# Attention scores over 64 rows, even and odd head back to back, with the attention pipeline stepped in pairs of units

## The reference

```
# layer 0 (DSA): 12 heads of 64, one shared k and v, mask "score" from an indexer
s = einsum('bthd,btkd->bthk', q, k) * 64 ** -0.5
p = masked_softmax(s, mask);  o = einsum('bthk,btkd->bthd', p, v)
# layer 1 (NSA): 12 heads in 2 groups, three branches for each head
o = g0 * att(q, k_cmp, v_cmp)      # 31 compressed keys
  + g1 * att(q_rot, k_s, v_s)      # causal, up to 512 keys
  + g2 * att(q_rot, k_w, v_w)      # causal, up to 512 keys
# both layers: 4 more heads over 256 memory positions
x = x + concat(tok, o_mem) @ w_o
```

## Time and profile before

| | |
|---|---|
| median of 3 runs | 3527.47 us (3523.74 to 3528.39) |
| profiled execution, its own time | 3527.51 us |
| span in its trace | 3525.7 us |
| PE busy in the span | 3348.1 us (95%) |
| DVE, ACT, POOL busy | 47%, 42%, 45% |
| attention of layer 0 | from 208.65 us to about 292 us |
| attention of layer 1 | from 857.8 us to about 1061 us |
| granted TensorE clock in both | 1.00 and 0.98 of full |

### The profile page before, as it was taken

How to read it: one execution, slowest core, us unless ns; L and a number is a source line. 1 busy time by engine, 2 the same in 40 slices (tenths; PEclk the granted TensorE clock), 3 DMA queues, 4 the chain that set the end, 5 groups by cost and what they waited for, 6 DMA issues and landing times.

```text
span 3525.7 us, 46614 instructions
## 1 busy us (share of the span) xinstructions
PE 3348.1 (95%) x16902; PEld 2768.0 (79%) x16902; DVE 1657.1 (47%) x2719; ACT 1472.4 (42%) x2771; POOL 1601.7 (45%) x1404
## 2 busy tenths in 40 slices
PE   6899999999999999999989996899999999999998
PEld 4578888877778888788877775788888878888886
DVE  4784433142773332343326876555565552333321
ACT  3355433223664333333325554454445542243322
POOL 4245544662445445544553321444444435464454
PEclk8899999997999999999999997999999999999999
DMA  4111333341002333333332220111111113333332
GB/s 122 42 43 49 95 95 97 94 115 37 1 1 84 95 95 94 95 98 95 94 86 62 59 54 25 37 43 37 42 37 37 39 46 96 96 96 95 98 96 70
DMA packets 471315, 245.93 MB, mean 70 GB/s; under 512 B 13820, under 2 KB 468711, under 8 KB 471015
## 3 DMA queue, kind: packets, MB, share of 16 engines
q1 hardware_dynamic: 470144, 241.33, 24.1%
q10 hardware_dynamic: 998, 2.30, 0.2%
HBM read 241.51 MB, written 2.10 MB: 69 GB/s over the span
## 4 chain that ended last, share of the span: by engine, by line
PE 85%; DVE 8%; ACT 3%; issue 2%; POOL 1%; DMA 0%; ACTq 0%; DVEq 0%; POOLq 0%
PE ps L463 18%; PE ps L464 18%; PE ps L465 18%; PE ps L1545 3%; PE ps L1525 3%; PE ps L2281 2%; PE ps L2177 2%; PE ps L2179 2%; PE ps L2178 2%; PE ps L2263 2%; PE ps L1534 2%; PE ps L1696 1%; PE ps L1697 1%; PE ps L1698 1%; PE ps L1769 1%
## 5 line engine op out<-in xcount | busy, mean ns | idle before, releaser
L445 POOL TENSOR_TENSOR w_lo<-ring,w_hi 128x512 fp32r<-128x512 f32 (+1 forms) x908 | 1223.8, 1369 | 1540.6 <-ACT w_hi L436 1540.6
L436 ACT ACTIVATE w_hi<-ring 128x512 fp32r<-128x512 f32 (+1 forms) x908 | 516.1, 617 | 1276.5 <-PE ps L465 1191.8
L463 PE MATMUL ps<-h_hi,w_hi 128*128 128x512 f32 x1776 | 701.7, 395 | 4.4 <-POOL w_lo L445 4.4
L465 PE MATMUL ps<-h_hi,w_lo 128*128 128x512 f32 x1776 | 691.9, 390 | 0.0
L464 PE MATMUL ps<-h_lo,w_hi 128*128 128x512 f32 x1640 | 638.8, 390 | 0.0
L463 PEld LDWEIGHTS ps<-h_hi,w_hi 128*128 128x128 f32 x1776 | 333.8, 188 | 80.7 <-POOL w_lo L445 6.4
L465 PEld LDWEIGHTS ps<-h_hi,w_lo 128*128 128x128 f32 x1776 | 333.7, 188 | 69.8
L464 PEld LDWEIGHTS ps<-h_lo,w_hi 128*128 128x128 f32 x1640 | 308.4, 188 | 68.5 <-issue 5.0
L464 PE MATMUL ps<-a_lo,w_hi 128*128 128x512 f32 x752 | 292.5, 389 | 0.0
L465 PE MATMUL ps<-a_hi,w_lo 128*128 128x512 f32 x720 | 280.1, 389 | 0.0
L463 PE MATMUL ps<-a_hi,w_hi 128*128 128x512 f32 x720 | 280.1, 389 | 0.0
(11 more groups left out here) (445 smaller groups left out, 6195.1 us busy)
## 6 DMA issues: line engine op xcount, KB each, us to landing
ring<-in_ffn_w_in SPq DMA_DIRECT2D x176, 512.0 KB, 3.8
ring<-in_w_in SPq DMA_DIRECT2D x96, 512.0 KB, 4.0
ring<-in_ffn_w_down SPq DMA_DIRECT2D x32, 512.0 KB, 3.7
ring<-in_ffn_w_out SPq DMA_DIRECT2D x32, 512.0 KB, 3.6
ring<-in_w_o SPq DMA_DIRECT2D x16, 512.0 KB, 3.7
ring<-in_w_branch_gdn SPq DMA_DIRECT2D x16, 512.0 KB, 3.6
ring<-in_nsa_w_in SPq DMA_DIRECT2D x15, 512.0 KB, 3.8
ring<-in_dsa_w_in SPq DMA_DIRECT2D x13, 512.0 KB, 4.1
```

The lines of the kernel that those rows point to most:

```text
L436: act.activation(w_hi[:, (halves(u) + j) % PIECES, 0:n, :], slot(u)[:, j * n:(j + 1) * n, :], ACT.Copy) \
L445: pool.tensor_tensor(w_lo[:, q % PIECES, 0:n, :], slot(u)[:, j * n:(j + 1) * n, :], w_hi[:, q % PIECES, 0:n, :].bitcast(f32), ALU.subtract ...
L463: pe.matmul(dst, wh, hi(k), start=first and k == 0, stop=False)
L465: ins = pe.matmul(dst, wl, hi(k), start=False, stop=last and k == 2 * n - 1)
```

## The change

On TensorE the contraction of a score product shrinks from 128 rows to the head's own 64 (`even_odd[n % 2]`), for all units, the compressed and the memory ones too. The even and the odd head of a pair are issued one right behind the other, so in layer 1 the order of units becomes: tile, branch, head. TensorE and ScalarE go on in steps of two units: TensorE's step i issues S of both units of pair-step i, T of both of i-2, and V of both of i-3, key tile by key tile, even and odd in turn; ScalarE's step i is both exponentials of i and then both copies of i-2. VectorE keeps its order unit by unit; only its copy out of a finished pair of heads comes later. The keys keep their zero rows, the values their padding, and no buffer or bank is added.

```
-    LEAD = 2
-            for t in range(NT):
-                for hh in range(2):
+            for t, br, hh in itertools.product(range(NT), range(1 if i == 0 else 3), range(2)):
...
     def pe_attention(pe, t, layer):
-        for n in range(N + LEAD + LAG_V):
-            if n < N:
-                u = us[n]
-                if n >= 4:
-                    pe.wait_ge(sig("att_masked").sem, t["masked"] + n - 3)
-                pe.matmul(ps[:, SCORE_BANKS[n % 4], 0:u["nk"]], u["q"], u["k"], start=True, stop=True) \
-                  .then_inc(sig("att_scores").sem, 1)
-            m = n - LEAD - LAG_T
...
-            m = n - LEAD - LAG_V
...
+        for i in range(N // 2 + LAG_V):
+            if i < N // 2:
+                if i >= 2:
+                    pe.wait_ge(sig("att_masked").sem, t["masked"] + 2 * i - 2)
+                for n in (2 * i, 2 * i + 1):
+                    u, rows_ = us[n], even_odd[n % 2]
+                    pe.matmul(ps[:, SCORE_BANKS[n % 4], 0:u["nk"]], u["q"][rows_], u["k"][rows_], start=True, stop=True) \
+                      .then_inc(sig("att_scores").sem, 1)
+            s = i - LAG_T
+            if 0 <= s < N // 2:
+                for m in (2 * s, 2 * s + 1):
+                    u = us[m]
+                    pe.wait_ge(sig("att_norm").sem, t["norm"] + m + 1)
+                    if m >= 2:
+                        pe.wait_ge(sig("att_copied").sem, t["copied"] + m - 1)
+                    for at, w in key_tiles(u):
+                        ins = pe.transpose(ps[0:w, 2 + m % 2, at:at + P], pr[:, m % DEEP, at:at + w], ident)
+                    ins.then_inc(sig("att_turned").sem, 1)
+            s = i - LAG_V
+            if 0 <= s < N // 2:
+                pe.wait_ge(sig("att_copied").sem, t["copied"] + 2 * s + 2)
...
+                for j, (at, w) in enumerate(tiles):
+                    for hh in range(2):
+                        u = us[2 * s + hh]
+                        ins = pe.matmul(ps[:, 4 + u["pair"] % 2, tok], u["v"][j], prT[0:w, hh, at:at + P],
...
     def dve_attention(dve, ch, t):
-            m = n - LAG_V - 2
+            m = n - 2 * LAG_V - 4
...
     def act_attention(act, t, layer):
+        for i in range(N // 2 + LAG_V + 1):
+            if i < N // 2:
+                for n in (2 * i, 2 * i + 1):
+                    u = us[n]
+                    act.wait_ge(sig("att_max").sem, t["max"] + n + 1)
+                    if n >= DEEP:
+                        act.wait_ge(sig("att_turned").sem, t["turned"] + n - DEEP + 1)
+                    act.activation(pr[:, n % DEEP, 0:u["nk"]], sm[:, n % DEEP, 0:u["nk"]], ACT.Exp,
...
+            s = i - LAG_T
+            if 0 <= s < N // 2:
+                for m in (2 * s, 2 * s + 1):
+                    u = us[m]
+                    act.wait_ge(sig("att_turned").sem, t["turned"] + m + 1)
+                    if m >= 2:
+                        act.wait_ge(sig("att_value").sem, t["value"] + m - 1)
...
+                    act.activation(prT[0:w, m % 2, 0:n_t], ps[0:w, 2 + m % 2, 0:n_t], ACT.Copy) \
+                       .then_inc(sig("att_copied").sem, 1)
```

More of the change, by code:

```diff
@@ L8 @@
 import numpy as np
+import itertools
 from concourse import mybir
@@ L1477, in units_of_layer @@
                     at = HD * (2 * g + 1 - hh)
[L1478 to L1487, removed]
+                    u = dict(gate=gates[:, t, 3 * h + br:3 * h + br + 1], out=tok, first=br == 0 and hh == 0,
+                             last=br == 2 and hh == 1, pair=pair, clamp=br == 0, need=0)
+                    if br == 0:
+                        u |= dict(q=q_raw[:, pair, tok], k=k_cmp[:, g, hh, 0:NC], bias=cmp_bias[:, t, 0:NC],
+                                  nk=NC, v=[v_cmp[0:NC, at:at + P]])
+                    else:
+                        u |= dict(q=q_rot[:, pair, tok], k=k_pad[:, br - 1, g, hh, 0:nk], bias=cb, nk=nk,
+                                  v=[v_tok[:, br - 1, j, at:at + P] for j in range(t + 1)])
+                    us.append(u)
         for pair in range(MEM_PAIRS):
@@ L1519, in pe_attention @@
         pe.wait_ge(sig("pads_zero").sem, (1, 4)[layer])
-        for n in range(N + LEAD + LAG_V):
-            if n < N:
-                u = us[n]
-                if n >= 4:
-                    pe.wait_ge(sig("att_masked").sem, t["masked"] + n - 3)
-                pe.matmul(ps[:, SCORE_BANKS[n % 4], 0:u["nk"]], u["q"], u["k"], start=True, stop=True) \
-                  .then_inc(sig("att_scores").sem, 1)
-            m = n - LEAD - LAG_T
[L1528 to L1535, removed]
-            m = n - LEAD - LAG_V
[L1537 to L1540, removed]
+        for i in range(N // 2 + LAG_V):
[19 more added lines that the diff above has]
+                pe.wait_ge(sig("att_copied").sem, t["copied"] + 2 * s + 2)
+                u = us[2 * s]
+                if u["pair"] >= 2 and (s == 0 or us[2 * s - 1]["pair"] != u["pair"]):
@@ L1544, in pe_attention @@
                 for j, (at, w) in enumerate(tiles):
-                    ins = pe.matmul(ps[:, 4 + u["pair"] % 2, tok], u["v"][j], prT[0:w, m % 2, at:at + P],
-                                    start=u["first"] and j == 0, stop=u["last"] and j == len(tiles) - 1)
-                ins.then_inc(sig("att_value").sem, 1)
+                    for hh in range(2):
+                        u = us[2 * s + hh]
+                        ins = pe.matmul(ps[:, 4 + u["pair"] % 2, tok], u["v"][j], prT[0:w, hh, at:at + P],
+                                        start=u["first"] and j == 0, stop=u["last"] and j == len(tiles) - 1,
+                                        skip_group_check=True)
+                        if j == len(tiles) - 1:
+                            ins.then_inc(sig("att_value").sem, 1)
     def dve_attention(dve, ch, t):
@@ L1551, in dve_attention @@
         need = 0
-        for n in range(len(us) + LAG_V + 3):
+        for n in range(len(us) + 2 * LAG_V + 5):
             if n < len(us):
@@ L1590, in act_attention @@
         N = len(us)
[L1591 to L1611, removed]
+        for i in range(N // 2 + LAG_V + 1):
[6 more added lines that the diff above has]
+                    act.activation(pr[:, n % DEEP, 0:u["nk"]], sm[:, n % DEEP, 0:u["nk"]], ACT.Exp,
+                                   bias=neg_max[:, n % 8:n % 8 + 1], accum_out=row_sum[:, n % 8:n % 8 + 1]) \
+                       .then_inc(sig("att_prob").sem, 1)
+            s = i - LAG_T
[5 more added lines that the diff above has]
+                        act.wait_ge(sig("att_value").sem, t["value"] + m - 1)
+                    w = min(P, u["nk"])
+                    n_t = len(key_tiles(u)) * P
+                    act.activation(prT[0:w, m % 2, 0:n_t], ps[0:w, 2 + m % 2, 0:n_t], ACT.Copy) \
+                       .then_inc(sig("att_copied").sem, 1)
+            m = 2 * (i - LAG_V) - 1
+            if 0 < m < N and (m == N - 1 or us[m + 1]["pair"] != us[m]["pair"]):
```

## The result

The changed kernel takes 3595.61 us (median of four, 3579.22 to 3597.91) against 3527.93 before: a ratio of 1.0187, 95% interval 1.0171 to 1.0203. It is slower, as forecast, but by 68 us and not by 27, and outside the range of 3532 to 3582. The lowest of the four, 3579.22, had a mean granted clock of 0.964, the others 0.956 to 0.958. The profiled execution is one of 3594.69 us with a span of 3592.9, 67.2 more than before.

The account below looks back on a forecast made before the run. PE bounded the kernel before; the change would make loops of copy waits the bound. Layer 0 6.5, memory 5.0 and layer 1 8.2 give 19.7 us, plus 7.5 for the clock: 27 more, 3554, range 3532 to 3582.

Parts of the forecast that it names:

- The loop over two pair-steps: Both attentions: without TensorE's two-unit lead, T and V wait for copies behind new exponentials; 19.7 us more without the clock.
- 6.5 + 7.5: Layer 0: 6.5 us more from a 12.96 us period against 11.88, plus 7.5 from clock drops at five of six gaps.
- 8.2 + 2.5 us: Layer 1: 8.2 us more from six head pairs 1.36 longer; memory pair-steps of 2.49 against 2.18, 5.0 more over 16.
- In layer 1 I work out gaps of 1.8 at most and take no drop.: Layer 1's clock term: PE gaps of at most 1.8 us, so no clock drop was added to the forecast.
- The end of the range: High end, 3582: all layer 0 gaps hit (1.5), one 1.5 us gap per layer 1 head pair (9), couplings (17).
- That makes 31.35 against 29.99.: Layer 1's head-pair period under the change against before: 1.36 us longer for each of six, 8.2 more.
- one detour: Layer 1, V of t = 3 in two steps running: second V waits behind the first, 6.4 us instead of 5.4.
- couplings between the two loops that I have not added: Interactions of the two loops, which only lengthen them; 17 us allowed in the high end only.
- the 30.4 under the 31.35: Layer 1's odd-step loop: DVE 11.2, exponentials 2.8, copies 4.0, wakes 0.6, T 1.3, V 5.6, S 4.9.
- The visit to the 64-row form: PE switching to 64-row score products and back: 0.2 us going in and 0.2 coming out, 0.40 a visit.
- the third rival: PE stays the bound and buffers ride out the loops: 6 x 0.53 + 6 x 1.7 = 13 less, 3514; chance 0.14.
- the blocks of 31-row products: Layer 1 value products: 31-row products visited 4 times instead of 8, 4 x 0.34 us less a head pair.

Follow-up runs that it names:

- e1: The changed kernel with TensorE issuing the scores one pair-step further ahead of the transposes and value products; 3533.78 us, ratio to before 1.0018.
- e5: The changed kernel with ScalarE's two copies of i-2 ahead of the two exponentials of i; 3533.21 us, ratio to before 1.0014.
- e2: The changed kernel with full 128-row score products, in the pair order of the change; 3582.97 us, ratio to before 1.0150.
- e4: The changed kernel with three unused extra products of 384 columns behind S of tile 0 in layer 0; 3587.72 us, ratio to before 1.0167.
- e9: e8 with VectorE's copy out of a finished head pair four units later in layer 1; 3576.13 us in one run.
- e13: e9 with one extra product in step 9 of layer 1's head pairs instead of two; 3570.56 us.
- e8: The changed kernel with unused extra products in layer 1, one in steps 5, 6 and 11 and two in step 9 of each head pair; 3571.43 us.
- e6: The kernel before with score products contracting 64 rows, unpaired, in the order of before; 3670.54 us, ratio to before 1.0405.
- e3: The changed kernel's 64-row score pairs and unit order, with TensorE's T and V lags and ScalarE's program of before; 3508.52 us, ratio to before 0.9941.
- e7: e3 with full 128-row score products in place of the row slices; 3523.03 us, ratio to before 0.9991.
- e14: e9 without the extra products of step 9, one each staying in steps 5, 6 and 11; 3573.98 us.

## Why the prediction was right and wrong

**The direction and the mechanism were right.** The loop over two pair-steps that the lost lead makes is what slowed the kernel. Its links stand in the timeline with the lengths forecast, undoing the lead on TensorE (e1) or the order on ScalarE (e5) brings 62 us back. Undoing the 64-row form (e2) brings 13, with 37 us less at half clock. That the loop of layer 0 hardly feels the overlap is shown too: 13.07 us without it (e2), 13.11 with it (e4, e9).

**Layer 0** was forecast at 6.5 + 7.5, and memory heads at 2.5 for each layer, 16.5 in all; it measured 20.3. The period of the loop was right (12.96 against 13.11). The clock's cost came out near by luck (7.5 against 8.8): each fall cost 2.2 and not 1.5, but there were four and not five. Memory pair-steps alternate between 2.1 and 2.9 us, 2.5 in the mean, as forecast. About 3 us lie behind the last scores, where three pair-steps instead of five units run out; that was not in the sum.

**Layer 1 is where it failed**, in two terms of the sum. It was forecast at 8.2 + 2.5 us and measured 46.4.

- "In layer 1 I work out gaps of 1.8 at most and take no drop." The gaps were as worked out, 1.8 at most, but the clock did fall: 65 us of that attention were at half clock, 8 before. The six head pairs took 219 us. With a first pair of 30.7, as in e13, and five of 33.2 at full clock, they would take 197. So this term, put at zero, was some 22 us. The end of the range had allowed 9 for it.
- "That makes 31.35 against 29.99." The loop was mis-sized: 33.2. I had added up each parity's loop and one detour. e9 shows that 0.40 was the copy-out on VectorE. For the remaining 1.5 the chain of e8 shows a path that changes between the parities over VectorE's masks and over PE; this is read from the chain, and no run isolates it. At full clock the head pairs would take 197 us against 178 before, so 19 us more and not 8.2: this term was some 11 us short, which "couplings between the two loops that I have not added" had only in the high end. (In the 30.4 under the 31.35, the terms as written give 10.9 for VectorE and not 11.2; with 10.9 the loop would have been 31.05, a little further off.)

The 2 us that are left of the 46.4 lie in the memory heads and behind the last scores, as in layer 0.

**The visit to the 64-row form** was put at 0.40 us; it measures 0.34, for a single product (e6, memory heads) and for a pair in layer 0 (e3 against e7), and 0.27 for a pair in layer 1. This hardly mattered for the forecast, but it made the third rival too small. Without the blocks of 31-row products, which e3 has not, its terms give 0.53 and 0.35 a head pair, 5 us in all, where the 64-row form won 15.7 us with TensorE as the bound (e3 against e7).

**The Trainium skill** (TensorEngine Tiling (Array Packing), Overview) gives up to 2x for a contraction of 64 or less. By that the estimate was 45 us less. The overlap is real, but of the 0.85 a tile-3 pair saves, a third goes into the visit, and the 15.7 us that are left (e3 against e7) show only where PE is the bound.

## What to carry to other kernels

When steps on several in-order engines are regrouped, count for each wait how many steps ago the work was issued that it hangs on, on every engine between, not only on the one whose program was shortened. A block of two in front of a queue delays what stands behind it by the whole block; in e5 two lines in the other order were worth 62 us. Where loops of different parity share an engine, one loop's sum can be too low (31.35 against 33.2 here): follow one whole period over all engines, and put the granted clock in as a term wherever PE is given new waits, even of 1 to 2 us.

## What the runs showed of the hardware

- Two float32 products over rows 0 to 63 and 64 to 127 start 6 or 7 ns apart (one pair of 112 in the change: 35), each with its two passes beside the other's, though they are issued one after the other (the four passes of 512 columns at 241.53 take 1.13 us).
- The length of a wait alone does not tell whether the clock falls. In layer 0 of the change it fell at four of five gaps of 2.4 to 2.63 us. In its layer 1 there are 25 waits of PE over 1 us and 10 stretches at half clock, each of which begins no later than 2.1 us behind such a wait. In e5 each of four waits of 0.88 us in layer 1 was followed, some 2 us later, by 3.4 us at half clock; in e8 six waits of 1.32 to 1.33, one a head pair, were followed by none.
- The clock can also fall, and stay down, with PE busy. In e6 PE had no waits to speak of (1.0 us of idle in the 284 us of layer 1's attention, all near its start), yet from 1094.6 on it ran 54.6 us at 1.2 GHz. In layer 0 it was at 1.2 GHz for 37.5 us on end, from 210.6 on, 2 us behind a wait of 2.7 us. The same instructions ran at 2.4 GHz in other head pairs. e3 has two stretches of 3.4 us in layer 1 with no wait over 0.35 us near them. What sets them off stays open; in the change, too, some of the 65 us in layer 1 may be of this kind, since no run separates them from those behind a gap.
- Extra products in a wait cost nothing while they end before it does (13.11 us a head pair of layer 0 with them in e4 and without them in e9), and gave back 18 us in layer 1's attention by holding the clock (e8), though two of them were too long by 1 us a head pair (e14).
- A product over 64 rows between products over 128 rows costs PE 0.34 us more than its columns (1.44 against 1.10 us a memory unit, e6 against before). Left unpaired, that made the kernel slower than zero rows did (13.72 against 11.88 us a head pair at full clock).
